# Output projection of the first two layers split around the last read-out, with its conditioning work and drains reordered

## The reference, cut to what matters

```python
for l in range(DEPTH):                       # layers 0 and 1
    mod = silu_c @ w_ada[l] + b_ada[l]       # 6 * 1024 values: shifts, scales, gates
    ...
    fx = fourier_mix(col(ux, OFF_FOURIER, FOURIER_W), w_four[l])
    ax, ac = attention_group(ux, uc, base_c, q_norm[l], k_norm[l], tabs, ctx_out)
    rx, rc = hgrn_group(ux, uc, base_c, lb_all[:, l], hg_norm[l], ctx_out)
    x = x + g_a * (jnp.concatenate([fx, ax, rx], axis=-1) @ w_out[l])
    x = x + g_f * swiglu(rmsnorm(x) * (1 + sc_f) + sh_f, w_gate[l], w_up[l], w_down[l])
    ...                                      # the same for ctx where l == 0
```

## Time and profile before

| | us |
|---|---|
| median of three runs (lowest, highest) | 2096.52 (2089.58, 2099.05) |
| the profiled execution | 2095.84 |
| its span, first to last instruction | 2093.7 |
| PE busy | 1806.5 (86%) |
| DVE busy | 1337.9 (64%) |
| ACT busy | 833.9 (40%) |
| mean granted clock of TensorE | 0.913 of full |

### The profile page before, as it was taken

How to read it: one execution, slowest core, us unless ns; L and a number is a source line. 1 busy time by engine, 2 the same in 40 slices (tenths; PEclk the granted TensorE clock), 3 DMA queues, 4 the chain that set the end, 5 groups by cost and what they waited for, 6 DMA issues and landing times.

```text
span 2093.7 us, 30849 instructions
## 1 busy us (share of the span) xinstructions
PE 1806.5 (86%) x12222; PEld 1626.0 (78%) x12222; DVE 1337.9 (64%) x2476; ACT 833.9 (40%) x1601; POOL 59.9 (3%) x133
## 2 busy tenths in 40 slices
PE   4799888889989998798677999877799989579997
PEld 2689667877877887697576998675799879569996
DVE  1436877458876566667675687757588874465554
ACT  2523742252311221435533444356444444445442
POOL 0000031000000000000020000000000000000000
PEclk8899887989999999898777999988899999799999
DMA  8463010145555564233214898631589845014653
GB/s 281 125 201 86 17 47 21 41 122 171 185 172 165 181 196 156 72 112 87 81 41 121 244 270 263 219 95 27 161 244 278 291 141 153 21 41 121 183 179 132
DMA packets 359118, 300.60 MB, mean 144 GB/s; under 512 B 8048, under 2 KB 333408, under 8 KB 358592
## 3 DMA queue, kind: packets, MB, share of 16 engines
q1 hardware_dynamic: 357584, 294.22, 46.0%
q0 software_dynamic: 1392, 4.42, 0.9%
HBM read 297.56 MB, written 1.05 MB: 143 GB/s over the span
## 4 chain that ended last, share of the span: by engine, by line
PE 70%; DVE 15%; ACT 6%; issue 5%; DMA 3%; SPq 0%; DVEq 0%; ACTq 0%; POOLq 0%
PE bank L842 67%; PE bank L856 3%; ACT whigh L1334 2%; DVE ACC L1778 2%; DVE wlow L1762 1%; DVE A L2184 1%; ACT PB L1504 1%; DVE A L1859 1%; DVE A L2061 1%; DVE HTL L1865 1%; DMA A<-in_w_ada 1%; DVE A L2170 1%; DMA raw<-in_w_up 1%; DMA AWH<-in_ada_w 1%; DMA X<-in_ctx 0%
## 5 line engine op out<-in xcount | busy, mean ns | idle before, releaser
L1762 DVE TENSOR_TENSOR wlow<-raw,whigh 128x2048 fp32r<-128x2048 f32 (+1 forms) x183 | 409.9, 2243 | 329.6 <-ACT whigh L1334 329.2
L1334 ACT ACTIVATE whigh<-raw 128x2048 fp32r<-128x2048 f32 (+1 forms) x183 | 343.1, 1877 | 566.7 <-PE bank L842 387.1
L842 PE MATMUL bank<-HTH,whigh 128*128 128x256 f32 (+1 forms) x1424 | 446.8, 314 | 12.5 <-DVE HTL L1865 12.5
L842 PE MATMUL bank<-HTL,whigh 128*128 128x256 f32 (+1 forms) x1424 | 442.1, 310 | 0.0
L842 PE MATMUL bank<-HTH,wlow 128*128 128x256 f32 (+1 forms) x1424 | 441.7, 310 | 0.0
L842 PE MATMUL bank<-whigh,HTH 128*128 128x256 f32 (+1 forms) x1008 | 296.6, 294 | 14.9 <-DVE HTL L1865 5.8
L842 PEld LDWEIGHTS bank<-HTH,whigh 128*128 128x128 f32 x1424 | 275.4, 193 | 26.2 <-issue 13.6
L842 PE MATMUL bank<-wlow,HTH 128*128 128x256 f32 (+1 forms) x1008 | 292.6, 290 | 0.0
L842 PE MATMUL bank<-whigh,HTL 128*128 128x256 f32 (+1 forms) x1008 | 292.2, 290 | 0.0
L842 PEld LDWEIGHTS bank<-HTH,wlow 128*128 128x128 f32 x1424 | 274.9, 193 | 13.6
L842 PEld LDWEIGHTS bank<-HTL,whigh 128*128 128x128 f32 x1424 | 275.4, 193 | 12.5
(11 more groups left out here) (216 smaller groups left out, 2243.9 us busy)
## 6 DMA issues: line engine op xcount, KB each, us to landing
raw<-in_ffn_w_in SPq DMA_DIRECT2D x88, 512.0 KB, 5.3
A<-in_ada_w SPq DMA_DIRECT2D x42, 1024.0 KB, 6.7
A<-in_w_ada SPq DMA_DIRECT2D x32, 1024.0 KB, 5.5
raw<-in_w_gate SPq DMA_DIRECT2D x44, 512.0 KB, 4.2
raw<-in_w_up SPq DMA_DIRECT2D x44, 512.0 KB, 5.8
raw<-in_ffn_w_out SPq DMA_DIRECT2D x20, 1024.0 KB, 5.0
raw<-in_w_in SPq DMA_DIRECT2D x18, 1024.0 KB, 6.1
raw<-in_w_down SPq DMA_DIRECT2D x18, 1024.0 KB, 5.2
```

Of the source, the lines that this page charges most:

```text
L842: return nc.tensor.matmul(out, lhsT, rhs, start=start, stop=stop, skip_group_check=True)
L1334: nc.scalar.activation(parts(loads[n])[0], raw_slot(loads[n]), ACT.Copy).then_inc(*made("split_high", loads[n]))
L1762: V.tensor_tensor(low, raw_slot(loads[n]), as_float(high), ALU.subtract).then_inc(*made("split_low", loads[n]))
```

## The change

- `project_out` on PE follows a list of jobs (load j, tile t), `out_jobs`. In layer 0 the context tiles of the first three loads come first (six jobs, called `whole`), then the last tiles are turned, then tiles 0 and 1 of these loads, then the fourth load for all four tiles. In layer 1 the first four jobs do their k tiles 0 to 5 first (`begun`), then the turns, then k tiles 6 and 7.
- ACT and DVE follow: the context tiles' inputs are written first in layer 0, `attended_low` comes ahead of `readout`, and in layer 0 DVE does four drains of the projection ahead of the X tiles' turns.
- A tile's readiness is waited for at its first job (`enter`), in all four layers.
- `gate_rows(l, "mix")` goes from before the projection out to the last column group but one of the projection in, in all four layers.
- `ada_plan`: 30 chunks in layer 0's feed-forward (35 before), 20 in layer 1's (17), 20 in layer 2's (18), and the last two loads of each stay free. No load has two chunks.
- In the feed-forward `late` holds a chunk's PE and ACT work back by two loads.
- The drains of an h on DVE come ahead of its last load's chunk and split, and PE opens the bank of each tile when it comes to that tile.
- In the recurrence DVE's `take_read` goes ahead of `gate_sum`.

```diff
@@ ada_plan
-        keys = [key for key in load_plan() if key[1] == l and key[0] in ("gu", "dn")][1:-1]
+        keys = [key for key in load_plan() if key[1] == l and key[0] in ("gu", "dn")][1:-2]
-    give(feed_forward(0, 35))
+    give(feed_forward(0, 30))
     give(scan(1, 6))
-    give(feed_forward(1, 17))
+    give(feed_forward(1, 20))
+def out_jobs(l):
+    n = len(out_loads(l))
+    if l:
+        return [(j, t) for j in range(n) for t in X_TILES]
+    return [(j, t) for tiles in (C_TILES, X_TILES) for j in range(n - 1) for t in tiles] + [(n - 1, t) for t in C_TILES + X_TILES]
@@ late, on PE and ACT
-                if last_load[0]:
-                    beside(*last_load[0])
-                last_load[0] = key
+                while len(held) >= by and held:
+                    beside(*held.pop(0))
+                    if key:
+                        break
+                if key:
+                    held.append(key)
@@ project, on PE and ACT
                     late(key)
+                    if at == len(col_groups(l)) - 2:
+                        gate_rows(l, "mix")
@@ project_out, on PE
+                if l == 0:
+                    fourier_out(l, 1)
+                    mixed_turns(l, C_TILES)
+                fourier_out(l, 0)
+                whole = [(j, t) for j, t in jobs if t in C_TILES and j < len(shape) - 1]
+                for j, t in whole:
+                    enter(t)
+                    pe.wait_ge(*drained("m", l, t, 0))
+                    some(j, t, range(8))
+                begun = [(j, t) for j, t in jobs if l == 1 and j < 2]
+                for j, t in begun:
+                    enter(t)
+                    some(j, t, range(6))
+                mixed_turns(l, X_TILES)
+                for j, t in begun:
+                    pe.wait_ge(*drained("m", l, t, 0))
+                    some(j, t, range(6, 8))
+                for j, t in jobs:
+                    if (j, t) not in whole + begun:
+                        enter(t)
+                        pe.wait_ge(*drained("m", l, t, 0))
+                        some(j, t, range(8))
@@ feed_forward, on PE
-                        ps = {t: open_bank("x2", l, half, h, t) for t in tiles_of(l, "ffn")}
+                        ps = {}
...
+                                if c == 0:
+                                    ps[t] = open_bank("x2", l, half, h, t)
@@ recurrence, on DVE
+                    if n and steps[n - 1][3]:
+                        take_read(n - 1)
                     if n + 2 < len(steps):
                         gate_sum(n + 2)
-                    if n and steps[n - 1][3]:
-                        take_read(n - 1)
@@ feed_forward, on DVE
                             key = ("dn", l, half, h, c)
+                            if c == len(down_chunks(l, half)) - 1:
+                                drain(half, h)
                             beside(*key)
                             if key != last_down(l):
                                 split(index[key] + HIGH)
-                        for t in tiles_of(l, "ffn"):
...
@@ the program, on DVE (ACT alike, without readout and project_out)
+                for g, tiles in out_parts(l):
+                    for t in tiles:
+                        attended_low(l, t)
+                    if l < 2:
+                        fourier_out(l, g)
+                        if g == 0:
+                            readout(l, (0, 1))
+                            if l == 0:
+                                project_out(l, out_jobs(l)[:4])
+                        for t in tiles:
                             mixed_turns(l, t)
-                project_out(l)
+                project_out(l, out_jobs(l)[4:] if l == 0 else out_jobs(l))
```

More of the change, by code:

```diff
@@ L1192, in recurrence, with mixed_turns @@
                 use_banks(*range(NBANKS))
-            def mixed_turns(l):
-                for t in [t for ts in readouts(l) for t in ts]:
+            def mixed_turns(l, tiles):
+                for t in tiles:
                     pe.wait_ge(*upto("mixed", l, t))
@@ L1213, in project_out, with enter, some @@
             def project_out(l):
-                for t in tiles_of(l, "ffn"):
+                jobs, shape, entered, banks_of = out_jobs(l), out_loads(l), set(), {}
+                def enter(t):
+                    if t in entered:
+                        return
+                    entered.add(t)
                     pe.wait_ge(*upto("attended_low", l, t))
                     if l < 2:
-                        pe.wait_ge(*drained("m", l, t, 0))
-                if l < 2:
-                    for g in range(2 if l == 0 else 1):
-                        pe.wait_ge(*drained("ff", l, g))
-                for j, (nk, nc_) in enumerate(out_loads(l)):
+                        pe.wait_ge(*drained("ff", l, t // 2))
+                def some(j, t, ks):
+                    nk, nc_ = shape[j]
                     key = ("wo", l, j)
@@ L1224, in project_out @@
                     wh, wl = (w.rearrange("p (k c) -> p k c", k=nk) for w in parts(key))
-                    for t in tiles_of(l, "ffn"):
-                        ps = open_bank("x1", l, j, t)
-                        r = slice(P * t, P * t + P)
-                        for k in range(nk):
-                            last = mm3(ps[:, 0:nc_], (HTH[:, k, r], HTL[:, k, r]), (wh[:, k, :], wl[:, k, :]), k == 0, k == nk - 1)
-                        last.then_inc(*made("product", "x1", l, j, t))
+                    if ks[0] == 0:
+                        banks_of[j, t] = open_bank("x1", l, j, t)
+                    ps = banks_of[j, t]
+                    r = slice(P * t, P * t + P)
+                    for k in ks:
+                        last = mm3(ps[:, 0:nc_], (HTH[:, k, r], HTL[:, k, r]), (wh[:, k, :], wl[:, k, :]), k == 0, k == nk - 1)
+                    if ks[-1] == nk - 1:
+                        last.then_inc(*made("product", "x1", l, j, t))
+                if l >= 2:
+                    for j, t in jobs:
+                        enter(t)
+                        some(j, t, range(shape[j][0]))
+                    return
+                if l == 0:
[15 more added lines that the diff above has]
+                    some(j, t, range(6, 8))
+                for j, t in jobs:
+                    if (j, t) not in whole + begun:
+                        enter(t)
+                        pe.wait_ge(*drained("m", l, t, 0))
+                        some(j, t, range(8))
             def feed_forward(l):
@@ L1312, in _ @@
                     recurrence(l)
-                    for g in range(2 if l == 0 else 1):
-                        fourier_out(l, g)
-                gate_rows(l, "mix")
-                if l < 2:
-                    mixed_turns(l)
                 project_out(l)
@@ L1338, in beside, with late @@
                     modulation(*c)
-            last_load = [None]
-            def late(key):
-                if last_load[0]:
-                    beside(*last_load[0])
-                last_load[0] = key
+            held = []
+            def late(key, by=1):
+                while len(held) >= by and held:
+                    beside(*held.pop(0))
+                    if key:
+                        break
+                if key:
+                    held.append(key)
             pending = []
@@ L2246, in low, with drain @@
                             .then_inc(*made("hidden", l, f))
+                    def drain(half, h):
+                        for t in tiles_of(l, "ffn"):
+                            i = cond_of_tile(t) if l < 2 else 0
+                            dve.wait_ge(*drained("g", l, "ffn", i, h))
+                            ps = take("x2", l, half, h, t)
+                            link(V.tensor_tensor(ps[:, :], ps[:, :], grow[:, i, 512 * h:512 * h + 512], ALU.mult))
+                            x = X[:, t, 512 * h:512 * h + 512]
+                            V.tensor_tensor(x, ps[:, :], x, ALU.add).then_inc(*made("drained_dve", "x2", l, half, h, t))
                     for f in fs:
@@ L2265, in feed_forward @@
                                 split(index[key] + HIGH)
-                        for t in tiles_of(l, "ffn"):
-                            i = cond_of_tile(t) if l < 2 else 0
-                            dve.wait_ge(*drained("g", l, "ffn", i, h))
-                            ps = take("x2", l, half, h, t)
-                            link(V.tensor_tensor(ps[:, :], ps[:, :], grow[:, i, 512 * h:512 * h + 512], ALU.mult))
-                            x = X[:, t, 512 * h:512 * h + 512]
-                            V.tensor_tensor(x, ps[:, :], x, ALU.add).then_inc(*made("drained_dve", "x2", l, half, h, t))
             dve.wait_ge(*upto("ident_in"))
```

68 lines of the change are left out of this document (31 added, 37 removed).

## The result

| | before | after |
|---|---|---|
| median of 15 runs, us (lowest, highest) | 2095.39 (2085.35, 2099.05) | 2084.02 (2074.09, 2091.51) |
| ratio to before, 95% interval | | 0.9949 (0.9932 to 0.9967) |
| the profiled execution, its span | 2095.84, 2093.7 | 2084.09, 2082.0 |

The change gains 11 us where I had forecast 40. The busy times of the page hardly tell why: PE had 1806.5 us before.

A forecast was written before the change was run, and what follows sets the result against it. PE, busy 86% of the span, was taken as the bound in most places. Terms -7.4 - 11.9 - 11.6 - 5.8 - 4.9 + 3.7 - 2.3 = -40.2 from 2095.84 gave 2055.6, forecast 2056, range 2044 to 2077.

The forecast's parts named there:

- Chunks in layers 1 and 2: Feed-forwards of layers 1 and 2: three and two more chunks cost nothing, a 2.33 us wait goes; -2.3 us.
- DMA engines are full: Rival, layers 1 and 2: a 270 GB/s ceiling makes each load 0.7 us longer, +28, 2084 us; chance 0.05.
- DVE becomes the bound: Rival, layers 1 and 2: unshrunk DVE waits stretch each load to 6.6 us, +53, 2109 us; chance 0.03.
- Layer 0's feed-forward: Waits at chunks (-7.4) and for X at the drains (-11.9) go, and half clock with them (-11.6 us).
- The clock term: Layer 0's feed-forward: without the waits PE's 23.23 us at half clock need half; -11.6 us, bounds 0 and -11.6.
- The hand-over of layer 0: Recurrence to output projection: earlier start -10.1, other terms +1.3, +3.7, -1.9, +1.2; sum -5.8 us, between -1 and -8.
- the fourth term: Layer 0's gate rows, moved into the projection in, where PE was said to have nothing to wait for: +3.7 us.
- The wait at the X turns: Layer 0's hand-over, a sign: no PE wait above 1 us when the X tiles are turned.
- The hand-over of layer 1: Recurrence to output projection: -8.1 + 2.4 + 2.0 = -3.7, with part of the half clock gone -4.9 us together.
- Layers 2 and 3: Gate rows move to where PE is busy, +2.0 each; earlier start -1.2 and -0.6, clock +1.5: sum +3.7 us.
- The wait before layer 2's projection: A sign: PE waits about 3 us before layer 2's output projection.
- the hand-overs give nothing: Rival: the projection's new order meets a new wait, 10.7 us are lost, 2067 us; chance 0.09.

The follow-up runs named there:

- later: The changed kernel, with SP issuing a chunk's load one weight load later, still one bank for the folds: 2055.48 us, ratio 0.9813.
- tb_half_bytes: two_banks, with half of the rows of each chunk's weights left out of the loads in layers 1 and 2's feed-forwards: 2054.10 us, ratio 0.9818.
- before_later: The kernel before the change, with only SP issuing a chunk's load one weight load later: 2087.52 us, ratio 0.998.
- before_ffn: The kernel before, plus the change's feed-forward parts and the later chunk loads, but old output projection, gate rows and recurrence: 2052.42 us, ratio 0.9819.
- combo3: later, gate rows behind attention (layers 0, 1) or ahead of output projection (2, 3), layer 1's first feed-forward splits behind DVE's drains: 2047.53 us, repeated 2047.88.
- two_banks: The changed kernel, with the chunks' folds in the feed-forwards using two banks in turn instead of one: 2078.10 us, ratio 0.9938.
- act_first: The changed kernel, with ACT copying a fold's result ahead of the same load's split in the feed-forwards: 2081.73 us, ratio 0.9956.
- by_one: The changed kernel, with folds held back by one load behind DVE's place instead of two: 2088.38 us, ratio 0.9989.
- late_by_one: later, with folds one load behind DVE instead of two: 2071.88 us, ratio 0.9908.

## Why the prediction was wrong, step by step

**The step that failed** is "Chunks in layers 1 and 2", put at -2.3: I counted PE's fold (0.6 us each) and DVE's sum, and took the weight loads' arrival as given. Measured: +11.3 and +13.4 us, 27.0 us off in the term, of the 28.5 by which the profiled execution missed 2055.6. How late a weight load comes behind a chunk's load stood in no term of the sum. `later` (2055.5, both stages at 198.9) shows that all of it hangs on where a chunk's load stands in SP's queue, and lands on the 2056 that I had forecast. That agreement is partly luck: the hand-overs gave some 7 us less than forecast, and the edit on SP gives something of its own (4 us to the kernel before). For the chunks I had followed the loads only as a sum of bytes, in a rival, and never to the load behind them.

**The rival "DMA engines are full"** named 2084, which is what was measured, and yet it is not what happens: it wanted a ceiling at 270 GB/s and a DMA share of 1. The share was 0.81 (0.94 in the densest 100 us), and `later` carries 286 GB/s there at 1.02 with PE at 100.00 of 100. The loads were late for their order, not for a ceiling at 270. The 2084 of this rival is a coincidence. That halving the bytes cures it too (tb_half_bytes) shows that bytes count in this case, as what stands ahead of a weight load.

**The rival "DVE becomes the bound"** fell with `later`: DVE's busy time unchanged, PE never waiting.

**Layer 0's feed-forward** (-7.4 - 11.9 - 11.6 = -30.9) was right: -32.8, and by itself the part of drains and clock came to -18.2 against -17.7 (with the reserve given there). The clock term, of which I was least sure, holds in full: no half clock in 382 us, though PE changes its bank at every product. So the rule of the Trainium skill that I had set against it ("TensorE: Matmul & The Clock Gate", "A second HAM failure mode: psum-queue depth-cycling") does not show in this kernel.

**The hand-over of layer 0** was to give -5.8. The parts: the start of the projection moved by -11.0 against -10.1; the fourth term, gate rows in the projection in, was 3.7 and came to 7.2 (187.93 to 195.09), for PE stands there for 3.41 us until DVE has emptied a bank of the queries (timeline of PE):

```profile
187.93 1.95 PE L859 MATMUL bank<-ident,modc 128*128 128x128 f32 x16
...
193.28 2.05 PE L859 MATMUL bank<-ident,modc 128*128 128x128 f32 x16 [3.41 <-DVE QHL L2020]
```

"Where PE has nothing to wait for" was wrong. With +1.4 and +1.1 behind it the sum is -11.0 + 7.2 + 1.4 + 1.1 = -1.3. The table above has +3.6 in place of 7.2, and with it -4.9; but its 203.9 is the highest of four traces of the old order (mean 202.3), and the twelve with the gate rows in the projection in have 207.1 to 211.1 there (mean 209.3). By the means of these traces, which differ in other places, the hand-over gave -2.4. The wait at the X turns is 0.87 us, below the 1 us that I had set. That the stretch ahead of the projection is 178.4 us in one trace of the old order and 182.1 in another (before_later), and 167.4 and 172.0 in the new one, sets how finely one pair of traces can be read here: to some 4 us.

**The hand-over of layer 1** (-4.9): against before_ffn, which has the old hand-over, the projection starts 8.5 us sooner (135.1 and 143.6), the gate rows make the projection in 2.2 longer (104.2 and 102.0), and projection and norm take 5.4 more (43.5 and 38.1): -0.9 in all. The begun jobs end only after the turns, and with them the loads `wo` 0 and 1, whose slots the first two loads of the feed-forward need. DVE stands at its split of the first (6.11 us idle) with four drains of the projection behind it, and the norm's turn waits 10.93 us where it waited 5.15 (timeline of PE, then DVE):

```profile
1099.26 3.68 PE L873 MATMUL bank<-ident,A 128*128 128x128 f32 x16 [10.93 <-DVE A L1896]
```
```profile
1087.42 2.29 DVE L1818 TENSOR_TENSOR wlow<-raw,whigh 128x2048 fp32r<-128x2048 f32 x1 [6.11 <-ACT whigh L1388]
1089.63 0.43 DVE L1957 TENSOR_TENSOR bank<-bank,grow 128x256 f32<-128x256 f32 x1
```

For layer 0 I had looked at such a slot; for layer 1 I had not. In combo3, where the splits stand behind the drains, the wait is 7.98 and the stage 3.0 us shorter. Against the trace of before the same stages come to -1.6 - 10.3 + 5.7 = -6.2, but 3.8 us of that are a shorter projection in that before_ffn has without the new hand-over (102.0 and 105.8).

**Layers 2 and 3** were to lose 3.7 and lost 7.6 (2.3 + 5.3; 6.3 by the means of the four and twelve traces). The wait before layer 2's projection is there as forecast:

```profile
1437.09 0.36 PE L859 MATMUL bank<-whigh,HTH 128*128 128x256 f32 x1 [3.31 <-DVE HTL L1988]
```

The rival "the hand-overs give nothing" (0.09) is thus nearer to what was measured than the -10.7 of my two terms: -1.3 and -0.9 by the stages, and nothing measurable by before_ffn. Both terms had a cost that I had left out, and the third, of layers 2 and 3, was too small. Against the whole miss this is the smaller part.

## What to carry to other kernels

A load that is moved or added must be followed to the load behind it in the same queue: count not bytes per stage but what stands ahead of the transfer that someone waits for, and let loads for which there is time go behind it. When a wait disappears and the stage keeps its length (two_banks, act_first, by_one), the releaser named in the profile was the messenger; look for what it had itself been waiting for. When a piece of work leaves a stretch with waits, the stretch that it enters must be read for banks that are held and slots that come free later, as closely as the one that it leaves.

## What the runs showed of the hardware

- The ten 1 MB weight loads of layer 1's stage took 8.9 us (median) from issue to landing in the changed kernel, where over half of the stage's weight loads were issued 0.6 us behind another 1 MB load of the same queue. They took 5.2 us in `later`, where the load ahead had 2.8 us of start at the least and mostly 4.4 or more, at nearly the same traffic (252 and 268 GB/s).
- A mean DMA share of 0.81 (0.94 in the densest 100 us) didn't mean that loads were in time, and a share of 1.02 at 286 GB/s didn't mean that they were late.
- Five waits before a fold, 4.4 us together (8.5 less the longest of 4.1), left the clock at full speed over 169 us; the one of 4.13 us had 6.6 us at half around its end. Shorter waits came with such a stretch too: 2.36 us in late_by_one and 1.67 us in the kernel before, but not the 2.11 us there. Timeline windows of the changed kernel, columns as in the earlier trace rows:

```profile
1114.00:1283.00 169.00, 162.74 (x1235) 156.16 (x1233) 136.54 (x207) 69.32 (x103) 0.00 (x0) 1.00 0.87 264
```
